# Final RMSNorm of an encoder block moved under the last expert of its expert layer

## What is computed

```python
def expert(args):
    idx_e, gate_e, wg, wu, wd = args
    xe = ht[idx_e]
    he = jax.nn.silu(xe @ wg) * (xe @ wu)
    return (he @ wd) * gate_e[:, None].astype(xe.dtype)
ye = lax.map(expert, (idx, gates, w_gate, w_up, w_down))
y = jnp.zeros_like(ht).at[idx.reshape(-1)].add(ye.reshape(-1, D))
...
x = x + gate2 * y
...
def _rmsnorm(x, g):
    y = xf * lax.rsqrt(jnp.mean(xf * xf, axis=-1, keepdims=True) + RMS_EPS)
    return (y * g)
```

## Time and profile before

| what | value |
| --- | --- |
| runs | 2512.14, 2506.05, 2505.75 us; median 2506.05 |
| profiled execution, its own time | 2510.3 us |
| its span, first to last instruction | 2508.6 us |
| PE busy | 2337.1 us (93%) |
| DVE, ACT, POOL busy | 1505.7, 1158.7, 443.6 us |
| granted TensorE clock, mean | 0.963 |

### The profile page before, as it was taken

How to read it: one execution, slowest core, us unless ns; L and a number is a source line. 1 busy time by engine, 2 the same in 40 slices (tenths; PEclk the granted TensorE clock), 3 DMA queues, 4 the chain that set the end, 5 groups by cost and what they waited for, 6 DMA issues and landing times. The chain is left out here.

```text
span 2508.6 us, 39214 instructions
## 1 busy us (share of the span) xinstructions
PE 2337.1 (93%) x15048; PEld 1810.9 (72%) x15048; DVE 1505.7 (60%) x1785; ACT 1158.7 (46%) x1296; POOL 443.6 (18%) x396
## 2 busy tenths in 40 slices
PE   5999998899898999989993999999999999999993
PEld 3777887777776777744452888888888888888883
DVE  4566212545543333311214889889888888888984
ACT  4232222222222333311112767777777777777772
POOL 6110202232221000011231011111101111111101
PEclk9999999999997999999996999999999999999997
DMA  7446531001001232164213999999999999999994
GB/s 279 151 149 178 152 94 44 19 19 36 19 32 60 72 93 72 38 237 170 109 59 133 381 372 386 384 384 382 384 385 383 391 384 383 386 384 385 384 376 152
DMA packets 266048, 556.95 MB, mean 222 GB/s; under 512 B 13256, under 2 KB 66605, under 8 KB 262861
## 3 DMA queue, kind: packets, MB, share of 16 engines
q1 hardware_dynamic: 256717, 530.15, 58.3%
q0 software_dynamic: 4608, 16.78, 2.6%
q10 hardware_dynamic: 4608, 8.39, 0.9%
HBM read 511.21 MB, written 44.07 MB: 221 GB/s over the span
## 5 line engine op out<-in xcount | busy, mean ns | idle before, releaser
L2417 PE MATMUL ps<-whigh,xeT 128*128 128x512 f32 x2048 | 655.8, 394 | 1.5 <-DVE xeT L2564 1.5
L2572 DVE TENSOR_TENSOR wlow<-hT,whigh 128x2048 fp32r<-128x2048 f32 x192 | 431.9, 2284 | 62.6 <-ACT whigh L2513 62.6
L2417 PEld LDWEIGHTS ps<-whigh,xeT 128*128 128x128 f32 x2048 | 385.2, 188 | 80.5 <-issue 1.9
L2417 PE MATMUL ps<-wlow,xeT 128*128 128x512 f32 x1024 | 399.1, 390 | 0.0
L2513 ACT ACTIVATE whigh<-hT 128x2048 fp32r<-128x2048 f32 x192 | 358.6, 1911 | 10.3 <-PE ps L2417 10.3
L2417 PE MATMUL ps<-whigh,hidT 128*128 128x512 f32 x1024 | 328.0, 391 | 1.5 <-DVE hidT L2601 1.5
L2572 DVE TENSOR_TENSOR wlow<-oaT,whigh 128x2048 fp32r<-128x2048 f32 x96 | 216.7, 2286 | 41.5 <-ACT whigh L2513 41.5
L2572 DVE TENSOR_TENSOR wlow<-obT,whigh 128x2048 fp32r<-128x2048 f32 x96 | 217.9, 2284 | 21.2 <-ACT whigh L2513 21.2
L2417 PEld LDWEIGHTS ps<-whigh,hidT 128*128 128x128 f32 x1024 | 192.2, 188 | 42.2 <-issue 1.7
L2417 PEld LDWEIGHTS ps<-wlow,xeT 128*128 128x128 f32 x1024 | 193.0, 188 | 37.9
L2513 ACT ACTIVATE whigh<-oaT 128x2048 fp32r<-128x2048 f32 x96 | 181.8, 1913 | 39.1 <-PEq L2404 21.8
(11 more groups left out here) (291 smaller groups left out, 3426.0 us busy)
## 6 DMA issues: line engine op xcount, KB each, us to landing
hT<-in_w_down SPq DMA_DIRECT2D x66, 1024.0 KB, 10.1
obT<-in_w_up SPq DMA_DIRECT2D x64, 1024.0 KB, 10.1
hT<-in_w_up SPq DMA_DIRECT2D x64, 1024.0 KB, 7.9
hT<-in_w_gate SPq DMA_DIRECT2D x62, 1024.0 KB, 10.9
oaT<-in_w_down SPq DMA_DIRECT2D x62, 1024.0 KB, 8.3
oaT<-in_w_gate SPq DMA_DIRECT2D x34, 1024.0 KB, 10.1
obT<-in_w_gate SPq DMA_DIRECT2D x32, 1024.0 KB, 8.2
oaT<-in_w_ada SPq DMA_DIRECT2D x20, 1024.0 KB, 7.6
```

The lines of the kernel that those rows point to most:

```text
L2417: mm = pe.matmul(out, lhs[x], rhs[y], start=start and i == 0, stop=stop and i == 2)
L2572: dve.tensor_tensor(wlow[slot][:, :], raw[(FIRST + x) % RAW_SLOTS], whigh[slot][:, :].bitcast(F32), ALU.subtract).then_inc(low_done, 1)
```

## The change

The phase `phase_finish` is gone. Its work is in `phase_experts`, in two parts. The 8 row tiles of `x2_dram` are loaded while the last expert still runs, into `raw` slots that its weights have left, two tiles to a slot, once the scatter of expert 14 has landed; they are squared, normalised and written to `y`, without the last expert's contribution. The 128 rows that the last expert adds to are wrong then. They are also gathered into `xe`; when `ye` is there, DVE adds it to `xe` on chip, the sum is normalised as one tile into `ye`, and an indirect DMA without add writes it over these rows of `y`, after all 8 plain writes have landed. The transpose of quarter 3 moves from before `("d", 3)` to between the two halves of `("d", 2)`, on PE, ACT and DVE.

```diff
 def phase_experts(nc, a, m, ps, x2_dram, h2_dram, raw, raw_in, y):
...
+        x3 = [raw[t // 2][:, (t % 2) * D_MODEL:(t % 2 + 1) * D_MODEL] for t in range(NT)]
+        junk, fg = raw[4][:, 0:D_MODEL], raw[4][:, D_MODEL:2 * D_MODEL]
+        LAST = 2 * len(TURNS_LAST)
...
             def _(sp):
                 loop(sp, body)
+                sp.wait_ge(scattered, 16 * (NE - 1))
+                for i in range(NT // 2):
+                    sp.wait_ge(low_done, (NE - 1) * NH + FIRST + LAST - RAW_SLOTS + i + 1)
+                    sp.dma_start(raw[i].rearrange("p (t c) -> p t c", t=2), x_v[i]).then_inc(x3_in[i], 16)
+                sp.wait_ge(low_done, (NE - 1) * NH + FIRST + LAST - RAW_SLOTS + 5)
+                sp.dma_start(fg, bass.AP(a["final_g"].tensor, 0, [[0, P], [1, D_MODEL]])).then_inc(fg_in, 16)
+                for t in range(NT):
+                    sp.wait_ge(y_done, t + 1)
+                    sp.dma_start(y_v[t], x3[t]).then_inc(y_out, 16)
+                sp.wait_ge(y_out, 16 * NT)
...
             def _(pool):
+                    if last:
+                        pool.indirect_dma_start(out=xe[:, :], out_offset=None, in_=x2_dram[:, :],
+                                                in_offset=bass.IndirectOffsetOnAxis(ap=tok_s[:, 0:1], axis=0)).then_inc(own_in, 16)
+                        for t in range(NT + 1):
+                            inverse(t)
+                        pool.wait_ge(y_out, 16 * NT)
+                        pool.wait_ge(own_ready, 1)
+                        pool.indirect_dma_start(out=y[:, :], out_offset=bass.IndirectOffsetOnAxis(ap=tok_s[:, 0:1], axis=0),
+                                                in_=ye[:, :], in_offset=None).then_inc(own_out, 16)
+                        pool.wait_ge(own_out, 16)
+                        return
...
-                        if half == 0 and (kind, n) == ("d", 3) and last:
+                        if half == 1 and (kind, n) == ("d", 2) and last:
                             turn_hidden(3)
...
             def _(act):
+                SQUARES = {LAST - 4: (0, 1, 2, 3), LAST - 3: (4, 5), LAST - 2: (6, 7)}
+                        for t in SQUARES.get(x, ()) if last else ():
+                            square(t, x3[t], x3_in[t // 2])
+                    if last:
+                        act.wait_ge(own_sum, 1)
+                        square(NT, xe[:, :], own_in)
...
             def _(dve):
+                MEANS = {LAST - 4: (0, 1), LAST - 3: (2, 3), LAST - 2: (4, 5), LAST - 1: (6, 7)}
+                NORMS = {LAST - 3: (0, 1), LAST - 2: (2, 3), LAST - 1: (4, 5, 6, 7)}
+                        for t in MEANS.get(x, ()) if last else ():
+                            mean(t)
+                        for t in NORMS.get(x, ()) if last else ():
+                            norm(t, x3[t], x3[t], y_done)
                     multiplied(dve, e, count - 1)
...
+                    if last:
+                        dve.wait_ge(own_in, 16)
+                        dve.wait_ge(ye_done, 1 + e + 1)
+                        dve.tensor_tensor(xe[:, :], xe[:, :], ye[:, :], ALU.add).then_inc(own_sum, 1)
+                        mean(NT)
+                        dve.wait_ge(own_sum, 1)
+                        norm(NT, ye[:, :], xe[:, :], own_ready)
...
-def phase_finish(nc, a, m, x2_dram, y):
```

More of the change, by code:

```diff
@@ L2280, in _, with phase_experts @@
                 st.settle()
-def phase_experts(nc, a, m, ps, x2_dram, h2_dram, raw, raw_in):
+def phase_experts(nc, a, m, ps, x2_dram, h2_dram, raw, raw_in, y):
     NH = 2 * len(TURNS)
@@ L2311, in phase_experts @@
         ye = sb("ye", [P, D_MODEL])
+        ssq = sb("ssq_f", [P, NT + 1])
+        ms = sb("ms_f", [P, NT + 1])
+        rinv = sb("rinv_f", [P, NT + 1])
+        x3 = [raw[t // 2][:, (t % 2) * D_MODEL:(t % 2 + 1) * D_MODEL] for t in range(NT)]
+        junk, fg = raw[4][:, 0:D_MODEL], raw[4][:, D_MODEL:2 * D_MODEL]
         high_done = sem("high_done")
@@ L2331, in phase_experts @@
         ye_free = sem("ye_free")
+        x3_in = [sem(f"x3_in{i}") for i in range(NT // 2)]
+        fg_in = sem("fg_in")
+        own_in = sem("own_in")
+        ssq_done = sem("ssq_done_f")
+        ms_done = sem("ms_done_f")
+        rinv_done = sem("rinv_done_f")
+        y_done = sem("y_done")
+        y_out = sem("y_out")
+        own_sum = sem("own_sum")
+        own_ready = sem("own_ready")
+        own_out = sem("own_out")
+        LAST = 2 * len(TURNS_LAST)
         def loop(eng, body):
@@ L2365, in _, with inverse @@
                 loop(sp, body)
+                sp.wait_ge(scattered, 16 * (NE - 1))
+                x_v = x2_dram.rearrange("(i t p) c -> i p t c", p=P, t=2)
+                y_v = y.rearrange("(t p) c -> t p c", p=P)
+                for i in range(NT // 2):
[7 more added lines that the diff above has]
+                sp.wait_ge(y_out, 16 * NT)
             @block.gpsimd
             def _(pool):
+                def inverse(t):
+                    pool.wait_ge(ms_done, t + 1)
+                    pool.tensor_tensor(rinv[:, t:t + 1], ms[:, t:t + 1], m["neghalf"][:, 0:1], ALU.pow).then_inc(rinv_done, 1)
                 def gather(e_tok, count):
@@ L2502, in _, with square @@
                 prime(act, silu_done)
+                SQUARES = {LAST - 4: (0, 1, 2, 3), LAST - 3: (4, 5), LAST - 2: (6, 7)}
+                def square(t, src, landed):
+                    act.wait_ge(landed, 16)
+                    act.wait_ge(low_done, (NE - 1) * NH + FIRST + LAST - RAW_SLOTS + 5)
+                    if t:
+                        act.wait_ge(ssq_done, t)
+                    act.activation(junk, src, ACT.Square, accum_out=ssq[:, t:t + 1]).then_inc(ssq_done, 1)
                 def tokens(half, bank, count):
@@ L2537, in body @@
                         t = {("u", 1): 0, ("g", 2): 1, ("g", 3): 2, ("g", 0): 3}.get((kind, n)) if half == 1 else None
-                        if last and half == 0 and (kind, n) == ("d", 3):
+                        if last and half == 1 and (kind, n) == ("d", 2):
                             t = 3
@@ L2560, in _, with mean, norm @@
                 prime(dve, hid_done, ye_done, hidT_low)
+                MEANS = {LAST - 4: (0, 1), LAST - 3: (2, 3), LAST - 2: (4, 5), LAST - 1: (6, 7)}
+                NORMS = {LAST - 3: (0, 1), LAST - 2: (2, 3), LAST - 1: (4, 5, 6, 7)}
+                def mean(t):
+                    dve.wait_ge(ssq_done, t + 1)
+                    dve.tensor_scalar(ms[:, t:t + 1], ssq[:, t:t + 1], 1.0 / D_MODEL, EPS, ALU.mult, ALU.add).then_inc(ms_done, 1)
+                def norm(t, dst, src, done):
+                    dve.wait_ge(rinv_done, t + 1)
+                    dve.wait_ge(fg_in, 16)
+                    dve.scalar_tensor_tensor(out=dst, in0=src, scalar=rinv[:, t:t + 1], in1=fg,
+                                             op0=ALU.mult, op1=ALU.mult).then_inc(done, 1)
                 def tokens(half, bank, count):
@@ L2613, in body @@
                                              op1=ALU.mult).then_inc(ye_done, 1)
-                loop(dve, body)
-def phase_finish(nc, a, m, x2_dram, y):
[L2620 to L2679, removed]
@@ L2715, in build @@
                 phase_route(nc, a, m, ps, late, x2_dram, h2_dram, raw, raw_in, x_in)
-        phase_experts(nc, a, m, ps, x2_dram, h2_dram, raw, raw_in)
-        phase_finish(nc, a, m, x2_dram, y)
+        phase_experts(nc, a, m, ps, x2_dram, h2_dram, raw, raw_in, y)
 def kernel(**inputs):
```

## The result

The changed kernel took 2488.68 us (median of six runs) against 2506.62 for the kernel before in the same comparison: ratio **0.992, 95% interval 0.9909 to 0.9931**. The forecast was 2487.0 us, in a range of 2483 to 2493, and faster. The median takes in one execution of 6413.1 us, which no profile here explains and which the ratio leaves out. The profiled execution took 2489.15 us, with a span of 2487.4.

A forecast was written before the change was run, and what follows sets the result against it. TensorE's time plus what follows its end bounds the kernel; afterwards DVE is later. 2474.4 + 6.0 + 0.8 + 5.4 + 3.0 = 2489.6, 19.0 us under the old span; 2506.05 - 19.0 = 2487.0 us, range 2483 to 2493.

The forecast's parts named there:

- The place: After TensorE's last matmul: only this part changes, 36.4 us from the start of `ye` to the end.
- DVE as the later engine: Before `ye`: eight norms of 1.28 us behind `hidT` end at 2474.4, 3.8 us after TensorE's end.
- From `ye` to the indirect write: After the norms: `ye`, add, square, mean, power and norm take 6.0 us, then 0.8 to the write's start.
- The indirect write: Write of the separate tile over its 128 rows: lands 5.4 us after its start, between 4.5 and 6.2.
- The end behind it: From the indirect write's landing to the kernel's end: GpSimd's drain and the meeting of engines, 3.0 us.
- (a): DVE's norms before `ye`: six powers hold DVE about 0.5 us each, 3 us in all; 2490.0 us, chance 0.15.
- (b): Kernel's end: drain short behind a plain write, which lands in 4.5 us; 22.6 us off, 2483.4 us, chance 0.12.
- (c): Row-tile loads late at the second pair: ACT holds the `hidT` copy, TensorE stands still; 2513.6 us or more, chance 0.05.

The follow-up runs named there:

- the repetition: The unaltered changed kernel measured again against the kernel before, beside two further versions on one chip: ratio 0.9915, 33.88 us from last SiLU to end.
- the two built on it: Changed kernel, first norm earlier, means two norms ahead, landing awaited on SP: 30.66 us from last SiLU to end; also last norm behind the sum: 29.46.

## Why the prediction was right

**The place.** All of the gain is behind TensorE's last matmul, as the chain of waits had said: with the transpose moved back TensorE ends 18.6 us after the SiLU, where before it was 18.5, and the stretch is 33.88 us all the same.

**DVE as the later engine.** Right, and shown by the move of the transpose, worth 1.7 us before and nothing after. `ye` started 20.1 us after the SiLU; the forecast was 20.8. The difference of 0.8 is about half the norms' pace: I counted 1.28 each, and two take 2.47, four 4.86, so about 1.2; the other half is that `hidT` was split 0.4 us earlier.

**From `ye` to the indirect write.** Forecast 6.8 us (6.0 plus 0.8), measured 6.84 (2473.63 to 2480.47). The add took 1.23 where I had taken 1.28.

**The indirect write.** The one term that both counts in the sum and lay outside its bounds: I took 5.4 us between 4.5 and 6.2, and it landed in 3.4. Neither the gather nor the adding scatter was a bound; a plain scatter to memory was faster than both. The plain writes too landed sooner than my 4.5 to 6.4, in 2.7 to 3.8 us; that changed nothing, since the last was down 2.9 us before the indirect write started.

**The end behind it.** 3.0 us forecast, 3.57 measured (2483.86 to 2487.43): GpSimd's sequencer needed nearly 0.5 us between the landing and the drain, against 0.1 before, and the drain took 2.86 instead of 2.67. Summed, -0.8, -2.0 and +0.6 make the 2.2 us by which the span, 2487.4, lies under the forecast of 2489.6.

**How near the number came.** The forecast median was 1.7 us below the measured one, while the end of the kernel came out 2.2 us shorter than the sum had it. That the median is so near is in part luck: between the two medians lie 17.9 us here and 23.6 in the repetition, around the 21.1 of the stretch, and, as far as the two profiles of the changed kernel tell, what differs lies ahead of the last SiLU.

**The rivals.** (a) fell: GpSimd's powers took one norm's length each (7.81 us for six), and no norm was longer for it (1.27 to 1.28 us). The Trainium skill's rule on the shared port (SBUF — State Buffer, "Who interferes with whom") holds here for GpSimd as the one that is blocked, but for one power. DVE was not blocked in its turn: in the run with the norm earlier norm 4 started at 2465.42 beside a power that had started before it, and took 1.29; there the measurement goes against the rule. The one power that was not held stands at the same place in that run and the two built on it: it started 0.05 us after norm 0 and took 0.56 us, as when alone, and that norm took 1.32. Both powers, from the run with the norm earlier:

```profile
2459.01 0.56 POOL L2402 TENSOR_TENSOR rinv_f<-ms_f,neghalf 128x1 f32<-128x1 f32 x1
...
2465.36 0.54 POOL L2402 TENSOR_TENSOR rinv_f<-ms_f,neghalf 128x1 f32<-128x1 f32 x1
```

What the holding does cost is a wait of the next norm, 0.44 us, where its mean comes too late. (b) fell as named: the drain was not short behind a plain write; the write was short, by 1.1 us under my lower bound. (c) did not happen: the loads landed 2.0 to 2.8 us later than I had put them, but each pair still 6.5 us before ACT wanted it, and `final_g`, at 2460.0, 3.8 us before the first norm. Held back, they cost 9.1 us, and the kernel was still 12 us better than before. The rival had the path wrong, though: in that run ACT waited for the first tile and not for the second pair, and `ye` was set by `final_g`, with TensorE done 5.1 us ahead of it.

## What to carry to other kernels

When work is moved under another stage, look at which engine then comes last to the hand-over: here it passed from TensorE to DVE, and an edit worth 1.7 us before was worth nothing after. Where two engines take turns (a small step on one, a long one on the other), order the small step two long ones ahead. And read single edits from a stretch between two fixed points of the trace, when the whole time varies more than they do.

## What the runs showed of the hardware that was not expected

An indirect write of 128 rows of 4 KB without an add landed 3.4 us after its issue and held GpSimd for 1.04 us; the adding scatter of the kernel before took 6.2 at its shortest and held it for 1.58. GpSimd's drain at the end of a block with indirect DMAs takes 2.6 to 2.9 us, and begun before the landing it still ends 1.4 us after it; what it does in that time no run here shows.
